# Attention scores of heads 4 to 15 as three products of high and low parts, low parts by GpSimd, keys turned three heads ahead

## What is computed

```python
def one_block(args):                     # 128 queries at a time
    q_blk, blk_idx = args
    s = jnp.einsum('bhqd,bhkd->bhqk', q_blk, k) * scale
    s = jnp.where(key_pos[None, :] <= query_pos[:, None], s, NEG_INF)
    p = jax.nn.softmax(s, axis=-1)
    return jnp.einsum('bhqk,bhkd->bhqd', p, v)
```

## Time and profile before

| | |
|---|---|
| median of three runs | 1700.16 us |
| the profiled execution | 1700.47 us |
| its span, first to last instruction | 1698.6 us |
| TensorE busy | 1678.5 us, 99% of the span |
| VectorE busy | 927.7 us, 55% |
| ScalarE busy | 701.3 us, 41% |
| GpSimd busy | 685.4 us, 40% |
| granted TensorE clock, mean | 1.00 (2.4 GHz) |

### The profile page before, as it was taken

The page is one execution under the profiler, slowest core; times in us unless marked ns, Lnnn a source line. Parts: engine busy times, 40 slices in busy tenths (PEclk is TensorE's granted clock), DMA queues, the critical chain, the costliest instruction groups (busy, mean ns, idle before and its releaser), DMA issues.

```text
span 1698.6 us, 22530 instructions
## 1 busy us (share of the span) xinstructions
PE 1678.5 (99%) x8690; PEld 1385.2 (82%) x8690; DVE 927.7 (55%) x1619; ACT 701.3 (41%) x1193; POOL 685.4 (40%) x320
## 2 busy tenths in 40 slices
PE   8999999999999999999999999999999999999999
PEld 6887888888888788789888888899766888888887
DVE  3877899677966759433551451148784427226211
ACT  3433254244244655434332342276864333333221
POOL 4333202403303232534475484424722255845842
DMA  9522235453545468314413413322201251341332
GB/s 252 101 75 75 75 113 162 116 160 120 171 124 155 134 227 288 102 62 124 145 42 112 149 49 104 92 80 71 75 1 39 74 161 62 99 141 58 99 100 74
DMA packets 241833, 189.60 MB, mean 112 GB/s; under 512 B 40512, under 2 KB 198848, under 8 KB 241728
## 3 DMA queue, kind: packets, MB, share of 16 engines
q1 hardware_dynamic: 239856, 182.79, 35.8%
q10 hardware_dynamic: 1872, 5.37, 1.0%
HBM read 168.73 MB, written 19.40 MB: 111 GB/s over the span
## 4 chain that ended last, share of the span: by engine, by line
PE 88%; DVE 7%; ACT 3%; issue 1%; DMA 0%; DVEq 0%; SPq 0%; ACTq 0%
PE ps L420 15%; PE ps L422 14%; PE ps L421 14%; PE ps L448 7%; PE ps L450 6%; PE ps L449 6%; PE ps L662 3%; PE ps L664 3%; PE ps L665 3%; PE ps L542 2%; PE ps L544 2%; PE ps L543 2%; PE ps L1048 1%; PE ps L1078 1%; DVE x_rows L2071 1%
## 5 line engine op out<-in xcount | busy, mean ns | idle before, releaser
L1275 POOL TENSOR_TENSOR w_lo<-w_raw,w_hi 128x1024 fp32r<-128x1024 f32 (+2 forms) x224 | 542.4, 2437 | 906.8 <-ACT w_hi L1455 869.8
L420 PE MATMUL ps<-a_hi,w_hi 128*128 128x512 f32 (+1 forms) x1184 | 442.1, 373 | 0.0
L421 PE MATMUL ps<-a_lo,w_hi 128*128 128x512 f32 (+1 forms) x1184 | 440.4, 372 | 0.0
L422 PE MATMUL ps<-a_hi,w_lo 128*128 128x512 f32 (+1 forms) x1184 | 440.3, 372 | 0.0
L1455 ACT ACTIVATE w_hi<-w_raw 128x1024 fp32r<-128x1024 f32 (+3 forms) x263 | 265.3, 1030 | 123.5 <-DMA w_raw<-in_ffn_w_gate_up_dram 43.1
L420 PEld LDWEIGHTS ps<-a_hi,w_hi 128*128 128x128 f32 x1184 | 223.0, 188 | 40.3 <-issue 1.9
L422 PEld LDWEIGHTS ps<-a_hi,w_lo 128*128 128x128 f32 x1184 | 223.0, 188 | 38.5
L421 PEld LDWEIGHTS ps<-a_lo,w_hi 128*128 128x128 f32 x1184 | 223.1, 188 | 38.4
L2615 DVE TENSOR_TENSOR ev<-ps,xh 128x512 f32<-128x512 f32 x44 | 30.4, 692 | 324.9 <-PE ps L422 293.6
L448 PE MATMUL ps<-w_hi,a_hi 128*128 128x512 f32 (+1 forms) x288 | 112.4, 390 | 1.0 <-DVE a_lo L1977 1.0
L450 PE MATMUL ps<-w_hi,a_lo 128*128 128x512 f32 (+1 forms) x288 | 111.4, 387 | 0.0
(11 more groups left out here) (390 smaller groups left out, 2817.5 us busy)
## 6 DMA issues: line engine op xcount, KB each, us to landing
w_raw<-in_ffn_w_gate_up_dram SPq DMA_DIRECT2D x88, 512.0 KB, 3.7
w_raw<-in_w_up_dram SPq DMA_DIRECT2D x44, 512.0 KB, 3.9
w_raw<-in_ffn_w_down_dram SPq DMA_DIRECT2D x28, 512.0 KB, 3.5
w_raw<-in_w_in_dram SPq DMA_DIRECT2D x20, 512.0 KB, 4.5
w_raw<-in_w_down_dram SPq DMA_DIRECT2D x20, 512.0 KB, 3.9
s_records<-stage SPq DMA_DIRECT2D x16, 544.0 KB, 5.3
w_raw<-in_ssm_w_glu_dram SPq DMA_DIRECT2D x16, 512.0 KB, 4.5
side_raw<-in_ffn_w_down_dram SPq DMA_DIRECT2D x16, 512.0 KB, 6.2
```

The costliest lines, as they stand in the source:

```text
L420: pe.matmul(bank, wh, xh_, start=first, stop=False)
L421: pe.matmul(bank, wh, xl_, start=False, stop=False)
L422: return pe.matmul(bank, wl, xh_, start=False, stop=last)
L1275: pool.tensor_tensor(lo, raw, w_hi[:, n % RING, 0:w].bitcast(F), ALU.subtract).then_inc(lo_made, 1)
```

## The change

From head 4 on, the scores are made as three products of high and low parts (lq_hi, lq_lo, lk_hi, lk_lo), like the large products. ScalarE makes the high part of the queries by a copy of its own, VectorE that of the keys; both still write the float32 rows, and GpSimd subtracts to get the low parts. The 32 rotary rows of the keys' high part are copied once per slot by ScalarE. TensorE waits for GpSimd's low parts ahead of each head's scores (`heads_low`).

`head_turn` is cut in two. The queries of head h + 2 are turned at t = 0 of loop h, ahead of the probabilities' first transposition and of `pair_out`; the keys of heads h + 3 and h + 4 are turned at t = 1 of odd loops h. `k_turned` moves to the odd loops with them, and from head 4 on it has four scalings in place of two. GpSimd's stream is written anew: groups 1 and 2, low parts of heads 4 and 5 and the keys of 6 and 7, group 3, the queries of 6 and 7, keys and queries of 8 and 9, and then one weight chunk of the output product ahead of each further pair of heads; its wait for the third inverse sums is gone.

```diff
--- before.py
+++ after.py
@@ -71,6 +71,7 @@
 PI_IN = float(np.nextafter(np.float32(np.pi), np.float32(0)))
 LATENT_ORDER = [(0, 0), (0, 1), (1, 0), (0, 2), (0, 3)] + [(1, c) for c in range(1, 4)]
 KDEEP = 4
+SPLIT_HEADS = 4
 N_CONST, N_TURNED, N_PARAM = 13, 8, 7
 XC = 2
 
@@ -216,6 +217,11 @@
         nrm = scratch("nrm", [P, 3, 3, HC, TT * HN], F, 89.5)
         rot = scratch("rot", [P, 2, NH, ROPE // 2], F, 104.25)
         lq_t = scratch("lq_t", [QK, 2, SEQ], F, 64)
+        lq_lo = scratch("lq_lo", [QK, 2, SEQ], R, 64)
+        lq_hi = scratch("lq_hi", [QK, 2, SEQ], R, 68)
+        lk_lo = scratch("lk_lo", [QK, KDEEP, SEQ], R, 56)
+        lk_hi = [scratch(f"lk_hi{i}", [QK, KDEEP // 2, SEQ], R, (92, 108.25)[i]) for i in range(2)]
+        kt_slot = lambda h: (lk_hi[h % KDEEP // 2][:, h % 2, :], lk_lo[:, h % KDEEP, :], lk_t[:, h % KDEEP, :])
         k_rope = rot[:, 0, 0:2 * TT, :].rearrange("p (t a) c -> p t (a c)", t=TT)
         TRI = P * TT * (TT + 1) // 2
         tri = lambda t: slice(P * t * (t + 1) // 2, P * (t + 1) * (t + 2) // 2)
@@ -295,6 +301,8 @@
         group_rows = sem("group_rows")
         qk_rows = sem("qk_rows")
         key_rope_made = sem("key_rope_made")
+        rope_high = sem("rope_high")
+        heads_low = sem("heads_low")
         pool_step = sem("pool_step")
         max_ready = sem("max_ready")
         prob_ready = sem("prob_ready")
@@ -351,6 +359,9 @@
 
         def rows_of(w, k0, kn, c0, cn):
             return w[k0 * P:(k0 + kn) * P, c0:c0 + cn].rearrange("(k p) c -> p k c", p=P)
+
+        def low_count(h):
+            return 4 * ((h - SPLIT_HEADS) // 2) + 3 + h % 2
 
         def pool_out(h):
             return xh[:, h // 2, (h % 2) * HALF:(h % 2) * HALF + HALF]
@@ -1016,19 +1027,29 @@
                     rows_by_tile(("kv_b", c), mla_w_kv_b_2, a_hi, a_lo, KVR // P, c * HALF, HALF, 2,
                                  wait_t=(lambda t: kv_split + t + 1) if c == 0 else None)
 
-            def head_turn(h):
+            def rows_normed(h):
                 pe.wait_ge(qk_rows, 2)
                 if h >= HN:
                     pe.wait_ge(group_rows, h // HN)
+
+            def query_turn(h):
+                rows_normed(h)
                 b = open_bank(("qt", h))
                 for t in range(TT):
                     m = pe.transpose(b[0:QK, t * P:t * P + P], q_n[:, t, h, :], ident[:, :])
                 close_bank(("qt", h), m)
+
+            def key_turn(h):
+                rows_normed(h)
+                b = open_bank(("kt", h))
+                for t in range(TT):
+                    m = pe.transpose(b[:, t * P:t * P + P], k_n[:, t, h:h + 2, :], ident[:, :])
+                close_bank(("kt", h), m)
+
+            def head_turn(h):
+                query_turn(h)
                 if h % 2 == 0:
-                    b = open_bank(("kt", h))
-                    for t in range(TT):
-                        m = pe.transpose(b[:, t * P:t * P + P], k_n[:, t, h:h + 2, :], ident[:, :])
-                    close_bank(("kt", h), m)
+                    key_turn(h)
 
             def key_rope_turn():
                 pe.wait_ge(key_rope_made, 1)
@@ -1044,9 +1065,18 @@
                         pe.wait_ge(*freed[bank_no[("kt", h)]])
                     if h == 0:
                         pe.wait_ge(*freed[bank_no["key_rope"]])
-                b = open_bank(("sc", h, t), freed_by=(prob_ready, h * TT + t + 1))
-                m = pe.matmul(b[:, 0:(t + 1) * P], lq_t[:, h % 2, t * P:t * P + P],
-                              lk_t[:, h % KDEEP, 0:(t + 1) * P], start=True, stop=True)
+                b = open_bank(("sc", h, t), freed_by=(prob_ready, h * TT + t + 1))[:, 0:(t + 1) * P]
+                rows, cols = slice(t * P, t * P + P), slice(0, (t + 1) * P)
+                if h < SPLIT_HEADS:
+                    m = pe.matmul(b, lq_t[:, h % 2, rows], lk_t[:, h % KDEEP, cols], start=True, stop=True)
+                else:
+                    if t == 0:
+                        pe.wait_ge(heads_low, low_count(h))
+                    q_hi, q_lo = lq_hi[:, h % 2, rows], lq_lo[:, h % 2, rows]
+                    k_hi, k_lo, _ = kt_slot(h)
+                    pe.matmul(b, q_hi, k_hi[:, cols], start=True, stop=False)
+                    pe.matmul(b, q_hi, k_lo[:, cols], start=False, stop=False)
+                    m = pe.matmul(b, q_lo, k_hi[:, cols], start=False, stop=True)
                 close_bank(("sc", h, t), m)
 
             def head_probs(h, t):
@@ -1101,9 +1131,13 @@
                         pair_out(h // 2 - 1)
                     if t == 0 and h == 0:
                         head_turn(2)
+                    if t == 0 and h >= 2 and h + 2 < NH:
+                        query_turn(h + 2)
                     head_probs(h, t)
-                    if t == 1 and h and h + 2 < NH:
-                        head_turn(h + 2)
+                    if t == 1 and h == 1:
+                        query_turn(3)
+                    if t == 1 and h % 2 and h + 3 < NH:
+                        key_turn(h + 3)
                     if t == TT - 1 and h % 2:
                         inverses(h // 2)
             rows_product(("w_o", 0), mla_w_o_2[0], a_hi, a_lo, KT, 0, HALF, 2, wait_k=lambda k: pair_split + k + 1,
@@ -1227,6 +1261,24 @@
                 step(rope_chunk(pool, c, q_rot[:, 0, :, :, :, :], step))
                 rope = q_n[:, :, rows, NOPE:]
                 pool.tensor_tensor(rope, rope, inverse(2, c, ROPE), ALU.mult).then_inc(group_rows, 1)
+
+            def query_low(h):
+
+                pool.wait_ge(*freed[bank_no[("qt", h)]])
+                s_ = h % 2
+                pool.tensor_tensor(lq_lo[:, s_, :], lq_t[:, s_, :], lq_hi[:, s_, :].bitcast(F), ALU.subtract)\
+                    .then_inc(heads_low, 1)
+
+            def keys_low(h):
+
+                pool.wait_ge(*freed[bank_no[("kt", h)]])
+                n = NOPE
+                if h < SPLIT_HEADS + KDEEP:
+                    pool.wait_ge(rope_high, 2)
+                    n = QK
+                for i in range(2):
+                    hi, lo, raw = (a[0:n] for a in kt_slot(h + i))
+                    pool.tensor_tensor(lo, raw, hi.bitcast(F), ALU.subtract).then_inc(heads_low, 1)
 
             def make_decays(b_):
 
@@ -1273,11 +1325,23 @@
                 if n in side_of:
                     lo, raw = side_lo[:, side_of[n], 0:w], side_raw[:, side_of[n], 0:w]
                 pool.tensor_tensor(lo, raw, w_hi[:, n % RING, 0:w].bitcast(F), ALU.subtract).then_inc(lo_made, 1)
-                if n == chunks_at[("q_b", HC - 1, 0)] + 1:
+                first = chunks_at[("q_b", HC - 1, 0)] + 1
+                if n == first:
                     pool.wait_ge(trig_ready, 1)
-                    for c in range(1, HC):
-                        head_group(c)
-                    pool.wait_ge(sum_inverse, HC - 1)
+                    head_group(1)
+                    head_group(2)
+                    keys_low(4)
+                    query_low(4)
+                    query_low(5)
+                    keys_low(6)
+                    head_group(3)
+                    query_low(6)
+                    query_low(7)
+                if first <= n < first + 4:
+                    for h in range(8 + 2 * (n - first), 10 + 2 * (n - first)):
+                        if h % 2 == 0:
+                            keys_low(h)
+                        query_low(h)
 
         @block.sync
         def _(sp):
@@ -1820,8 +1884,13 @@
 
             def q_turned(h):
 
-                release(("qt", h), act.activation(lq_t[:, h % 2, :], at(("qt", h))[0:QK, :], ACT.Copy,
-                                                  scale=gcol[0:QK, 0:1]))
+                b = at(("qt", h))[0:QK, :]
+                if h >= SPLIT_HEADS:
+                    act.activation(lq_hi[:, h % 2, :], b, ACT.Copy, scale=gcol[0:QK, 0:1])
+                release(("qt", h), act.activation(lq_t[:, h % 2, :], b, ACT.Copy, scale=gcol[0:QK, 0:1]))
+                if h in (2, 3):
+                    act.activation(lk_hi[h - 2][NOPE:QK, :, :], lk_t[NOPE:QK, 2 * (h - 2):2 * (h - 1), :], ACT.Copy)\
+                       .then_inc(rope_high, 1)
 
             def key_rope_rows():
 
@@ -2710,6 +2779,10 @@
             def k_turned(h):
 
                 b = full(v, ("kt", h))
+                if h >= SPLIT_HEADS:
+                    for i in range(2):
+                        r = slice(NOPE * i, NOPE * i + NOPE)
+                        go(v.tensor_scalar(kt_slot(h + i)[0][0:NOPE], b[r, :], gcol[r, 1:2], None, ALU.mult))
                 go(v.tensor_scalar(lk_t[0:NOPE, h % KDEEP, :], b[0:NOPE, :], gcol[0:NOPE, 1:2], None, ALU.mult))
                 release(("kt", h), v.tensor_scalar(lk_t[0:NOPE, (h + 1) % KDEEP, :], b[NOPE:P, :],
                                                    gcol[NOPE:P, 1:2], None, ALU.mult))
@@ -2779,8 +2852,10 @@
                     if t == 2 and h % 2:
                         inverse_sums(h // 2)
                     if t == 1:
```

(6 more changed lines are left out.)

## The result

The kernel after takes 1733.45 us (median of four runs, 1732.86 to 1734.97) against 1700.13 us for the kernel before in the same session. The ratio is 1.0198, with an interval of 1.0185 to 1.021. The change makes the kernel slower by 33.3 us, 9.7 more than the 23.6 that the forecast of 1723.7 lies above the median of before, and 1.5 above the 1732 up to which it gave 8 chances in 10. The profiled execution took 1733.51 us with a span of 1731.7.

A forecast was written before the change was run, and what follows sets the result against it. The bound was taken as a VectorE-TensorE loop of 11.61 us per pair, growing to 14.06. Lateness of 13.9 us at loop 6, plus 10.4, less 1.1, gave 23.2 on 1700.47: 1723.7 us; 8 in 10 for 1714.5 to 1732.

The forecast's parts named there:

- The bound now: Attention, one pair of heads: a loop through VectorE (7.83 us) and TensorE with latencies (3.78) sets the 11.61 us period.
- parts 1 and 2: Per pair: four key scalings ahead of the inverse copy add 1.97 us; the query turn ahead of the output product, 0.44.
- Part 3: Scores of heads 4 to 15: three split products save 0.26 us a head, mostly into waiting; the chain gains +0.04.
- Part 4: ScalarE: one more 0.68 us copy per head and two copies of rope rows cost nothing at a 14 us period.
- Part 5: GpSimd's third head group (10.03 us) delays head 6's scores to 1246.0; 13.9 us late at loop 6's output product.
- the sum: Whole attention: 13.9 us late by loop 6, three pairs add 10.4, the pair of loops 12 and 13 -1.1; 23.2 us.
- Part 6: Loops 7, 9, 11: VectorE's inverse copy and a GpSimd weight chunk exclude each other; the copy waits some 1.0 us each.
- The clock falls: TensorE at 1.2 GHz from loop 5 to 11, behind new idle: +4 us in three or four pairs, 1737 us; chance 0.12.
- a clock under 1.00: Listed sign that the forecast is wrong: TensorE's granted clock below 1.00 (2.4 GHz).
- The end: The pair of loops 12 and 13 has no scalings: -1.15 + 0.04 = -1.1 us; the last pair keeps its time.

The follow-up runs named there:

- the kernel with the shorter wait: Kernel after with GpSimd's weight chunks of loops 7, 9 and 11 held back until the inverse copy is done: 1729.73 us, ratio 1.0165.

## Why the prediction was right in sign and wrong in size

- **The bound now and parts 1 and 2: right.** VectorE's order sets the pair. 14.06 us were worked out; 13.94 were measured where neither clock nor collision disturbed it (loops 4 and 5 with the group in pieces), 14.89 with the collision against 15.06. With two scalings 12.37 against 12.46.
- **Part 3, the split products: right.** Their spacing is 0.23 us at 512 columns and 0.11 at 128, as taken, and the 0.53 us a pair fell into waits, as said.
- **Part 4, ScalarE: right for this kernel.** The remark that "if the chain were shorter by 3 us they would be next" fits the small waits for low queries once the keys were late.
- **Part 5, the third group: the mechanism right, its place in the sum not.** A subtraction takes 1.27 us (1.29 taken), the group 10.01. The scores of head 6 started at 1247.64 (1246.0). Loop 2 started at 1220.30 (1220.2), but that closeness is luck: a collision of 0.9 us in loop 1 was missing in the forecast, and the execution was 0.70 us ahead when the attention began. But TensorE waited 2.1 us, not 5.5, since loops 2 to 4 were already late by the clock and by collisions. With the clock kept up the wait is 4.50. Cutting the group brought 4.6 us.
- **Part 6, the collision: right in size, too few of them.** A copy beside GpSimd took 1.37 us instead of 0.43, so 0.94 for the 1.0 taken. The sum has three of them. The trace has five: the copies of loops 1 and 3 took 1.34 and 1.64 us, 2.1 us more than the sum holds. The rule of the Trainium skill, page "SBUF — State Buffer", section "Who interferes with whom", that the port pair is locked for whole instructions, agrees with the copies that met one operation (1.34 and 1.37 us). It doesn't tell when a copy gets in between two operations of GpSimd, as with 1.34, and when it waits through the second as well, as with 1.64 and 2.57.
- **The rival "The clock falls": this step failed.** The prediction gave it a chance of 0.12, and in the range one fall at 2 us; the sum has nothing for it. The ground was that the clock stood at 1.00 in the first 10 us with TensorE busy 3.4. That row was a false witness, as the spacing of the products in the same trace would have told. TensorE's order of time at the start of the kernel before:

```profile
9.10 0.63 PE L449 MATMUL ps<-w_lo,a_hi 128*128 128x512 f32 x1
9.53 0.63 PE L450 MATMUL ps<-w_hi,a_lo 128*128 128x512 f32 x1
...
15.32 0.40 PE L449 MATMUL ps<-w_lo,a_hi 128*128 128x512 f32 x1
15.56 0.40 PE L450 MATMUL ps<-w_hi,a_lo 128*128 128x512 f32 x1
```

and of the kernel after:

```profile
12.29 0.63 PE L461 MATMUL ps<-w_hi,a_lo 128*128 128x512 f32 x1
...
13.07 0.39 PE L460 MATMUL ps<-w_lo,a_hi 128*128 128x512 f32 x1
13.30 0.39 PE L461 MATMUL ps<-w_hi,a_lo 128*128 128x512 f32 x1
```

The products of 512 columns are 0.43 us apart until 13.8 us before and until 12.7 us after, and 0.23 apart from then on, while the clock's column says 1.00 throughout. So TensorE was slow behind its idle start, and the row that spoke against the rival speaks for it. (That the step comes at another moment in each execution is also where the 0.70 us of head start come from.) The rival named the right waits, "over 5 us ahead of loop 5 and 2 to 3 in each odd loop", and the prediction listed "a clock under 1.00" as a sign of being wrong; what failed is that this clock was held to be unlikely and put at nothing. Its price of +4 in three or four pairs was too high, since the clock was down for only part of each: 1.6, 1.6 and 2.4 us in the three pairs from loop 6 on, and some before. The Trainium skill, "TensorE: Matmul & The Clock Gate", Part 1, says that the engine drops to half rate behind an idle spell. The windows of 0.56 and 0.53 behind the wait of 3.21 us agree, but not every wait here was followed by a fall: none came behind one of 3.19 us with float32 scores and one of 2.27 us with the pieces.
- **The end: a small miss, and another wait for GpSimd.** The pair of loops 12 and 13 was to give back 1.1 us and gave back none. VectorE's inverse copy did come 1.2 us sooner in it (6.14 us behind C against 7.35), but the scores of head 15 then had to wait for their low queries:

```profile
1319.64 0.30 PE L1077 MATMUL ps<-lk_hi,lq_hi 96*128 96x128 f32 x1 [0.72 <-POOL lq_lo L1269]
```

- **The sum again.** 23.2 forecast, 2.1 for two more collisions, 1.1 for the end and 7.4 for the clock: 33.8, and the attention took 33.8 us longer. The 7.4 is from a run, the 2.1 and the 1.1 from rows; that they add up that well is partly luck, as the price of the clock includes what it did to the wait for the third group.

## What to carry to other kernels

Where two engines take turns, find the instruction on the second one on which the first waits, and count everything that a change puts ahead of it; work that can stand behind it costs little (17.3 us here for the place of the four scalings and of the key turn ahead of them). A forecast that creates waits of some microseconds on TensorE must price its clock at each of them, and check the clock's column by the spacing of equal products. Faster products showed no gain here, where the engine waits for others.

## What was not expected of the hardware

- Useless transposes made the kernel faster by 7.4 us: the clock stayed at 1.00 in the pairs from loop 6 on, and was down to 0.90 and 0.80 in such pairs without them.
- Taking 0.94 us out of a wait of 3.21 did not keep the clock up. With a wait of 2.27 us the pair had a mean clock of 0.80, lower than the 0.90 with the longer wait, while with the group in pieces a wait of the same 2.27 us left it at 1.00. The runs of the kernel with the shorter wait spread over 11 us, those of the others over 1 to 3, and 7.6 in the one with early query copies. So the length of a single wait doesn't tell whether and how far the clock falls, and what does is left open.
- The clock's column said 1.00 in the first 13 us, before and after, while equal products were 0.43 us apart in place of 0.23.
- A VectorE copy that met two GpSimd subtractions in a row took 2.57 us, that is it waited through both; another, begun as early beside the same two, took 1.34 and was done in the midst of the second.
